# GpSimd makes the last quarter of the low parts of each expert step's down weights

## The reference

```python
def swiglu(h, w_gate, w_up, w_down):
    return (jax.nn.silu(h @ w_gate) * (h @ w_up)) @ w_down
...
logits = (t @ w_router).astype(jnp.float32)
top_val, top_idx = lax.top_k(logits, TOP_K)              # TOP_K = 2
top_w = jax.nn.softmax(top_val, axis=-1)
gates = jnp.sum(jax.nn.one_hot(top_idx, N_EXPERTS) * top_w[..., None], axis=1)
y = jnp.zeros_like(t)
for e in range(N_EXPERTS):                               # 8 experts, 1024 -> 3584 -> 1024
    y = y + gates[:, e:e + 1] * swiglu(t, w_gate[e], w_up[e], w_down[e])
```

## Time and profile before

| | us |
|---|---|
| median of 3 runs (1403.98 to 1405.41) | 1404.4 |
| the profiled execution | 1404.34 |
| its span, first to last instruction | 1402.6 |

### The profile page before, as it was taken

One profiled execution on the slowest core, in us unless ns is written; L12 is line 12 of the kernel. 1 busy time (PEld: TensorE's weight loads), 2 busy tenths in 40 slices (PEclk: granted clock), 3 DMA queues, 4 the chain that ended last, 5 costly groups with the idle time before them and its releaser, 6 DMA issues. The chain is left out here.

```text
span 1402.6 us, 16576 instructions
## 1 busy us (share of the span) xinstructions
PE 1360.6 (97%) x6286; PEld 1097.0 (78%) x6286; DVE 1127.3 (80%) x1317; ACT 948.5 (68%) x1262; POOL 124.4 (9%) x124
## 2 busy tenths in 40 slices
PE   7999999999999999999999999999999999999997
PEld 4885788886786678878877888787787888877885
DVE  3565445553655599999999999999999999999895
ACT  4544534443545287887887879788788878888782
POOL 2041000001031111400000010300000010000100
PEclk9999999999999999999999999999999999999999
DMA  9333555528124499999999999999999999999992
GB/s 358 121 113 143 209 189 185 195 74 305 34 87 180 162 399 391 391 402 403 399 398 390 384 400 403 398 401 400 399 398 404 402 396 399 399 402 401 403 390 104
DMA packets 157128, 435.24 MB, mean 310 GB/s; under 512 B 5556, under 2 KB 10356, under 8 KB 148980
## 3 DMA queue, kind: packets, MB, share of 16 engines
q1 hardware_dynamic: 153988, 423.11, 79.2%
q0 software_dynamic: 3056, 11.02, 2.0%
HBM read 428.33 MB, written 5.78 MB: 310 GB/s over the span
## 5 line engine op out<-in xcount | busy, mean ns | idle before, releaser
L2110 DVE TENSOR_TENSOR unit_rounded<-wmem,unit_rounded 128x1024 fp32r<-128x1024 f32 (+1 forms) x744 | 852.2, 1206 | 50.0 <-ACT unit_rounded L1495 48.9
L1495 ACT ACTIVATE unit_rounded<-wmem 128x1024 fp32r<-128x1024 f32 (+1 forms) x744 | 720.4, 1044 | 143.1 <-PE ps L1033 45.9
L1031 PE MATMUL ps<-unit_rounded,vbuf_rounded 128*128 128x512 f32 x416 | 162.8, 391 | 0.0
L1033 PE MATMUL ps<-unit_rounded,stage_rounded 128*128 128x512 f32 x416 | 162.5, 391 | 0.0
L1032 PE MATMUL ps<-unit_rounded,vbuf_rounded 128*128 128x512 f32 x416 | 162.5, 391 | 0.0
L1169 PE MATMUL ps<-unit_rounded,hT_rounded 128*128 128x512 f32 x336 | 135.3, 403 | 0.0
L1169 PE MATMUL ps<-unit_rounded,qkT_rounded 128*128 128x512 f32 x336 | 133.3, 397 | 1.4 <-DVE qkT_rounded L2307 1.4
L1171 PE MATMUL ps<-unit_rounded,hT_rounded 128*128 128x512 f32 x336 | 132.6, 395 | 0.0
L1170 PE MATMUL ps<-unit_rounded,hT_rounded 128*128 128x512 f32 x336 | 132.4, 394 | 0.0
L1171 PE MATMUL ps<-unit_rounded,qkT_rounded 128*128 128x512 f32 x336 | 131.0, 390 | 0.0
L1170 PE MATMUL ps<-unit_rounded,qkT_rounded 128*128 128x512 f32 x336 | 130.9, 390 | 0.0
(11 more groups left out here) (288 smaller groups left out, 1942.7 us busy)
## 6 DMA issues: line engine op xcount, KB each, us to landing
wmem<-in_w_exp_gate_dram SPq DMA_DIRECT2D x56, 2048.0 KB, 14.9
wmem<-in_w_exp_up_dram SPq DMA_DIRECT2D x56, 2048.0 KB, 15.7
wmem<-in_w_exp_down_dram SPq DMA_DIRECT2D x56, 2048.0 KB, 15.9
wmem<-in_w_in_dram SPq DMA_DIRECT2D x4, 3072.0 KB, 17.2
wmem<-in_w_ff_up_dram SPq DMA_DIRECT2D x5, 2048.0 KB, 9.0
wmem<-in_w_ff_gate_dram SPq DMA_DIRECT2D x5, 2048.0 KB, 8.0
wmem<-in_w_ff_down_dram SPq DMA_DIRECT2D x5, 2048.0 KB, 8.2
wmem<-in_w_out_dram SPq DMA_DIRECT2D x4, 2048.0 KB, 7.9
```

The source lines that it names most:

```text
L1031: pe.matmul(o, hhb, hi[:, b, c], start=(first and b == 0), stop=False, skip_group_check=True)
L1033: mm = pe.matmul(o, hlb, hi[:, b, c], start=False, stop=(b == blocks - 1), skip_group_check=True)
L1495: act.activation(quarter_r(HIGH[l][0 if last else kind], q, cols), quarter(SETS[l][i][kind], q, cols), ACT.Copy).then_inc(hi_ready[kind], 1)
L2110: dve.tensor_tensor(quarter_r(u, q, cols), quarter(u, q, cols), quarter_r(HIGH[l][0 if last else kind], q, cols), ALU.subtract).then_inc(l ...
```

## The change

POOL gets a function `low_part(m)`: it waits for ACT's fourth high part of the down weights of step m and makes the fourth low part, with a count of its own, `last_low`. DVE makes the other three, in all steps but the last, in which it still makes four. PE waits for `last_low` ahead of the fourth block of `down` and `few_down`; the values that it waits for on `lo_ready[2]` count three a step. On POOL, `low_part(m)` stands in each step behind its gather and keep; the first round of fetches is issued in step 53 ahead of `low_part(53)`, the second behind `low_part(54)`. The DVE waits and additions that use them are not moved. The same is done in the path for all tokens (`parts` and `whole` below), which isn't taken here.

```diff
+        last_low = sem("last_low_down_part_ready")
...
-            def down(l, i, step, bufs, t, cols, done, count, first=False, part_of=None):
+            def low_parts(l, step):
+                return step * QUARTERS if l == 0 else step * (QUARTERS - 1) + DENSE_STEPS
+
+            def down(l, i, step, bufs, t, cols, done, count, first=False, part_of=None, whole=False):
...
-                        if t == 0 and (half == 0 or blocks < QUARTERS):
-                            pe.wait_ge(lo_ready[2], step * QUARTERS + (part + 1))
+                        if t == 0 and half == 0 and b == blocks - 1 and l and not whole:
+                            pe.wait_ge(last_low, step - (DENSE_STEPS - 1))
+                        elif t == 0 and (half == 0 or blocks < QUARTERS):
+                            pe.wait_ge(lo_ready[2], low_parts(l, step) + (part + 1))
...
                 for b in range(FT // P):
-                    pe.wait_ge(lo_ready[2], step * QUARTERS + b + 1)
+                    if b < FT // P - 1:
+                        pe.wait_ge(lo_ready[2], low_parts(1, step) + b + 1)
+                    else:
+                        pe.wait_ge(last_low, m + 1)
...
+            def low_part(m):
+                i, q = m % 2, QUARTERS - 1
+                pool.wait_ge(hi_ready[2], (DENSE_STEPS + m) * QUARTERS + q + 1)
+                u = SETS[1][i][2]
+                pool.tensor_tensor(quarter_r(u, q, FT), quarter(u, q, FT), quarter_r(HIGH[1][2], q, FT), ALU.subtract) \
+                    .then_inc(last_low, 1)
+
+            def pick(t):
+                if t:
+                    pool.wait_ge(s_pick, 16 * 2)
+                    pool.wait_ge(pick_added, 1)
+                else:
+                    pool.wait_ge(s_kept, 16 * (E - 1))
+                    pool.wait_ge(pos_ready, 1)
+                for j in range(2):
+                    pool.indirect_dma_start(xs[:, j, :], None, kept, bass.IndirectOffsetOnAxis(ap=spot[:, j, t:t + 1], axis=0)) \
+                        .then_inc(s_pick, 16)
+
             for m in range(MOE_STEPS):
                 for n in range(1, E):
                     if m == INDEX_AT[n]:
                         gather(n)
                 if m in READ_AT:
                     keep(READ_AT[m])
-            pool.wait_ge(s_kept, 16 * (E - 1))
...
+                if m == MOE_STEPS - 3:
+                    pick(0)
+                if m + 1 < MOE_STEPS:
+                    low_part(m)
+                else:
+                    pick(1)
             pool.wait_ge(s_pick, 16 * 2 * NT)
...
-            def low(l, i, kind, step, cols=FT, last=False):
-                for q in range(QUARTERS):
+            def low(l, i, kind, step, cols=FT, last=False, parts=QUARTERS):
+                for q in range(parts):
...
                     if m + 1 < MOE_STEPS:
-                        low(1, i, 2, step)
+                        low(1, i, 2, step, parts=QUARTERS - 1)
```

More of the change, by code:

```diff
@@ L1066, in one @@
                         return
-                    down(l, i, step, 0, 0, cols, step * 2 + 1, 1, first=(s == 0))
+                    down(l, i, step, 0, 0, cols, step * 2 + 1, 1, first=(s == 0), whole=(s == n - 1))
                     transposes(1, cols, step * 2 + 2, 1)
@@ L2136, in one @@
                     hidden_scaled(scale(0), 0, step * 2 + 1, cols)
-                    low(l, i, 2, step, cols)
+                    low(l, i, 2, step, cols, parts=QUARTERS - 1 if l and s != n - 1 else QUARTERS)
                     hidden_low(0, step * 2 + 1, 1, cols)
```

## The result

The changed kernel took 1440.7 us (median of 4 runs, 1438.5 to 1441.9) against 1404.3 for the kernel before (1404.0 to 1405.4): ratio 1.0247, 95% interval 1.0235 to 1.0259. That is 36.4 us more, where 35 were forecast. The profiled execution has a span of 1438.9 us against 1402.6.

A forecast was written before the change was run, and what follows sets the result against it. PE and DVE were taken as both full and balanced in the middle, DVE becoming slower with the change. 27 (middle) + 1 (GpSimd's queue) + 7 (tail) = +35 us on 1404.34 gave 1439, range 1413 to 1465.

The forecast's parts named there:

- -51 us of work: Middle, 560 to 1280 us: one of 12 low parts leaves DVE, 1.14 us a step in 45 steps.
- +27 in the middle: 45 steps at +0.86 us net on DVE, 39 us, of which some 12 use up DVE's idle time.
- +1 for GpSimd's queue: Moved part behind two long gathers: PE waits 3 us twice; +1 us counted for both (0 to 6).
- +7 at the tail: Second row fetch stands behind `low_part(54)`, so DVE waits 7 us for the rows (3 to 9).
- The size of GpSimd's subtraction: 128x1024 on GpSimd: 2.0 us from 1.78 ns a column, bounds 1.8 and 2.54.
- That the two exclude each other: A two-input DVE instruction and a GpSimd instruction reading SBUF block each other throughout; a moved part holds DVE 2.0 us (1.5 to 2.5).
- the two take turns, whole instruction by whole instruction: GpSimd gets in at the end of DVE's running low part and holds the next; its instruction lasts 2 to 3.5 us.
- wrong: PE waiting for the last quarter itself in more than the two steps named: Sign against the forecast: PE waits for GpSimd's part in more steps than the two behind the long gathers.
- Rival A: Turns don't bind; DVE saves up to 1.14 us a step, PE's waits shrink: -14 us, 1390; chance 9%.
- No DVE idle time.: Sign for the forecast: DVE has no idle time from 560 us to the end of step 49.
- Waits at the small steps' transposes.: Sign for the forecast: PE waits 3 to 5 us there, with slow clock behind most.

The follow-up runs named there:

- The memset: Changed kernel with a write-only GpSimd fill in place of its subtraction in steps 0 to 50, fourth low part left out of the matmuls: 1410.4 us, 1.0039.
- The small kernels: Four separate kernels: rows of two-input DVE parts, one GpSimd subtraction asked at a chosen point; no such subtraction over 3.42 us, total times say nothing.
- Removal alone: Changed kernel with GpSimd making no low part, PE reading the high part again for the fourth, fetches as before: 1398.4 us, 0.9951.
- the kernel where nobody waits for GpSimd: Changed kernel, GpSimd subtracting on its own tiles in steps 0 to 50 with nobody waiting, fourth part left out, fetches as before: 1418.3 us, 1.0091.
- the first experiment: Changed kernel with the second round of row fetches issued ahead of GpSimd's low part of step 54 instead of behind it: 1431.6 us, 1.0196.
- `pick(1)` first: Changed kernel with the second fetch of the tokens' rows ahead of `low_part(54)`: 1431.6 us, 1.0196.
- with four parts on DVE: Kernel before, DVE making all four parts, plus an unneeded GpSimd subtraction on its own tiles in steps 0 to 50, nobody waiting: 1476.0 us, 1.0500.

## Why the prediction was right

**The total is right (1440.7 for 1439), but in part by luck: in the middle two errors cancelled.** The forecast was -51 us of work, DVE the bound, +27 in the middle, +1 for GpSimd's queue, +7 at the tail.

- *The size of GpSimd's subtraction.* 2.0 us forecast from 1.78 ns a column, within 1.8 to 2.54. Alone it takes 2.34, the shortest in the kernel is 2.37. The linear reading of two small sizes was 15% low.
- *That the two exclude each other.* Right, down to the place: of the four parts at 600.50 one is held by 2.2 us. The Trainium skill, page "SBUF — State Buffer", section "Who interferes with whom", has the same rule, and adds that a GpSimd instruction that only writes does not contend with a two-input DVE instruction. The memset (0.96 us, DVE held 0.6 us beside 51 of them) agrees.
- *The step that failed: "the two take turns, whole instruction by whole instruction".* The small kernels do, the real one doesn't: DVE passes GpSimd over by up to ten parts. Hence two errors of opposite sign. The hold was put at 2.0 us a part and is 1.43, and of the low parts near 3.2 us, one in eleven by the forecast, there are seven (over 3 us) in the whole run. PE's wait for the last quarter was put at two steps and +1 us, and is 13.3 us in ten steps. Two of those are the ones behind the long gathers that I named (PE stops 1.6 us each, 3 forecast). The other eight come from passing over, and "wrong: PE waiting for the last quarter itself in more than the two steps named" came true. Mostly they fall in small steps, where PE comes to the fourth quarter soonest.
- *The removal.* It stands in my sum at -1.14 us for each part, on the assumption that DVE is the bound all through the middle. Removal alone gives 7 us in all and 2.4 by step 54; by the waits of that trace ACT and the transfers behind it are next in line. I saw "only ACT feels" the 398 GB/s and did not ask when DVE would feel ACT. Rival A's 1390 lies below even the kernel that has no fourth part at all (1398).
- *"No DVE idle time."* Wrong: 33 us. With TensorE stopped by GpSimd, DVE waits for ACT, 31.7 us from 486 to 1430 us; in the kernel where nobody waits for GpSimd, DVE idles 18.7 us in the window (720 - 701.27).
- *The middle.* +27 forecast, +28.2 measured at step 54: -2.4 (removal), +20.2 (hold), +10.4 (late GpSimd). DVE's share was forecast at 27 and is 17.8; GpSimd's lateness, of which 1 was forecast, made up for it. That the two cancel is luck: the sum is right by size and only in part by mechanism.
- *Waits at the small steps' transposes.* 3 to 5 us with slow clock forecast. PE's stops there are 0.6 to 3.2 us, 17.8 us in 13 stops, against 13.6 in nine before, so this was forecast too high. Behind the longer stops of PE the granted clock fell, behind shorter ones it fell or stayed (window, PE busy, granted clock, DMA):
```profile
746.30:750.30 4.00, 4.00 (x12) 0.50 1.10 438
1148.20:1152.20 4.00, 3.96 (x12) 0.50 1.05 388
...
595.50:599.50 4.00, 3.97 (x19) 1.00 1.04 396
812.50:816.50 4.00, 3.98 (x12) 0.61 1.05 388
```
  They follow stops of 3.2, 2.4, 1.6 (this one in `few_down`, for GpSimd) and 1.6 us. At 0.50 TensorE is at 1.2 GHz and makes 12 matmuls in 4 us instead of 19.
- *The tail.* +7 forecast, 7.4 measured, and the first experiment takes it away by order alone. The way there differs a little: GpSimd was passed over twice instead of holding DVE for 2.0 us, so DVE was ready sooner and waited 9.0 us.

Open: what decides whether a waiting GpSimd gets in at the next boundary. Neither a PSUM read ahead, idle time, satisfied waits, ACT's copies, transfers, matmuls nor writing in place brings passing over about in the small kernels; combinations and patterns that I haven't built remain (in the small kernels each DVE part shares at least one input tile with the next, for one). That the late GpSimd costs 10.4 us is a difference of two kernels, and includes what PE's stops do to the clock.

No version beat the kernel before but the one that leaves the part out. The best with the whole computation is `pick(1)` first, at 1431.6.

## What to carry to other kernels

Price a subtraction on GpSimd by what DVE loses, not by GpSimd's own idle time: here 2.34 us of GpSimd for 1.14 us of DVE, with DVE held for 1.4 to 2.2; none of the orders tried made it pay. When work is taken from a full engine, ask first what feeds it: "DVE 98% busy" hid ACT and the transfers just behind, and 45 us freed were worth 2 to 7. And a moved step takes its place in a queue: look at what was issued early from there (the fetches of the tokens' rows) and keep it ahead.

## What was not expected of the hardware

- A GpSimd instruction that reads SBUF can be passed over by a run of two-input DVE instructions: by six of the seven parts from 518.47 on, by ten in the longest instruction of the changed kernel (14.7 us); with four parts on DVE the longest lasts 25.6 us. The Trainium skill, page "SBUF — State Buffer", section "Who interferes with whom", says that issue order decides who blocks. The small kernels agree (next boundary, 3.36 us for the held part), the trace of the changed kernel doesn't: six DVE parts started after GpSimd had asked, as far as the start of its instruction in the profile tells when it asked.
- A turn that GpSimd does get costs DVE 2.15 us for 1024 columns and 0.13 for 64, nearly the whole GpSimd instruction less some 0.19.
- DVE's tiny one-input copy (0.14 us) lets nobody in where two-input parts follow it at once (ten of ten places), while a PSUM read of 0.68 us did at 526.41 (and one of 0.67 us at 940.03 did not).
